# Turning the first inverse by 32x32 blocks on VectorE instead of on TensorE, with GpSimd filling its unit matrices

## The chip, the cores and the metric

The kernel runs on one core of one Trainium2 chip. A core has five engines that work side by side, each through its own list of instructions: TensorE (PE, matrix products, with a separate weight load PEld), VectorE (DVE), ScalarE (ACT), GpSimd (POOL) and SyncE (SP), which here issues the loads. They meet only at semaphores: an instruction may wait for a count and may raise one when it is done. The metric is the device time of one execution in microseconds (us), the median of several.

## The reference

Two transformer blocks run one after the other on a 256 x 1024 input. The change lies in the second block, in its gated delta rule. There each value head, for each block of tokens, needs the inverse of a unit lower triangular matrix:

```python
kb = k * beta[..., None]
A = jnp.where(strict, jnp.einsum('bhntk,bhnsk->bhnts', kb, k) * Lmat, 0.0)
T = lax.linalg.triangular_solve(eye + A, jnp.broadcast_to(eye, A.shape),
                                left_side=True, lower=True, unit_diagonal=True)
u = jnp.matmul(T, v * beta[..., None])
w = jnp.matmul(T, kb * jnp.exp(gam)[..., None])
```

The two blocks are otherwise large matrix products (`w_in`, `ffn` and so on), in single precision.

## The kernel before

Every large product is done on TensorE in three passes. ScalarE writes the high part of a weight chunk (`w_hi`, L655), VectorE the remainder (`w_lo`, L1241), and TensorE multiplies high by high, high by low and low by high. Weights arrive in chunks of 128 x 2048 numbers in a ring of three slots; SyncE refills a slot once `lo_ready` says that it was split.

The second block's heads are worked in a loop, `head(i, gemm, main)`: once for i = 0 without the "main" part, then seven times in a loop that each engine runs for itself (`Fori(1, GH)`), then once more without the "gemm" part. In one pass TensorE computes the projections of head i (24 pieces called `quarter(n)`) and strews between them the small matrix work of head i-1 (`main`). The order on each engine is the order in which the code is written; there is no scheduler.

The inverse is built by doubling. `nt` is the negated strict lower triangle times its decay, for two token blocks and two value heads (128 x 512 numbers together). Level 0 takes from it the pairs directly below the diagonal, the 2x2 blocks:

- VectorE writes four unit matrices into `yi` (L1977), and later, with `copy_predicated` under the mask `lmask[0]`, puts the level-0 entries of `nt` into it (L2007). A `drain` behind it raises `y0_ready` (L2008).
- TensorE waits for `y0_ready` between `quarter(21)` and `quarter(22)` and turns the four 128x128 matrices of `yi` into the PSUM bank `M[:, 5]` (L2967, `t_done`).
- ScalarE copies this bank to `xi` (L1193, `t_ready`) and the diagonal quarters of it to `xc` (L1195, `xc_ready`). Before that it copies quarters of `nt` to `ntc` (L1189, `ntc_ready`).
- VectorE in the meantime, behind L2007, writes the low part of a weight chunk in two halves (L1241), does the prefix sums (L2014), the decayed keys (L2015, L1796), `mt` (L2020), and multiplies the scores into `lt` (L2024), which raises `lt2_ready`. Then it copies the token bank from PSUM (L2028, `evac[1]`).
- At the start of its next pass TensorE waits in `inv_z(1)` for `t_ready`, `ntc_ready` and `lt2_ready` together (L2802 and the lines ahead of it), and its first products read `xi` and `ntc` (L2812).

The steps that lead to L2000 on VectorE, the first of that matrix work: TensorE turns the first mixer's output (L2898); ScalarE works that off (L1154), then key lengths, scaled values, the delta rule's output norm and the query lengths, and the exponential of `lt` (L1165, which waits for `lt_pre` from L1988 on VectorE and raises `lt_ready`); VectorE waits for `lt_ready` at L2000. `vn1_done` is raised by TensorE at L2912, the last product that reads `yi` in a pass.

GpSimd builds masks at the start, writes one `w_lo` chunk halfway, and has nothing else to do.

Of the kernel before, what the change touches and what calls it, by code (L numbers as in the profile page):

```python
# [13 lines left out]
P = 128  # L14
T = 256
TT = T // P
# [67 lines left out]
def emit(nc, ctx, a, out):  # L84
# [3 lines left out]
    def sem(name):  # L88
        return ctx.enter_context(nc.semaphore(name))
# [189 lines left out]
    def quad(ap, side):  # L279
        return ap[HD * side:HD * side + HD, :, :, HD * side:HD * side + HD].rearrange("p i e c -> p (i e) c")  # L280

    def kept(ap, side):
        return ap[HD * side:HD * side + HD, :, :, :].rearrange("p i e c -> p (i e) c")
# [4 lines left out]
    def yh_bank(tile):  # L288
        if tile < 4:
# [62 lines left out]
                         "gbc_ready", "gam_done", "lt_pre", "lt_ready"))  # L352
    qk_done, y0_ready, t_done, t_ready, ffn_step = (
        sem(n) for n in ("qk_done", "y0_ready", "t_done", "t_ready", "ffn_step"))
    zz_done, zc_ready, ww_done, wt_done, xx_ready, yy_ready, yt_done, xc_ready, ntc_ready = (
# [5 lines left out]
        sem(n) for n in ("gsq_ready", "gss_done", "grs_ready", "ogh_ready", "ogl_ready"))  # L361

    gate_tanh = sem("gate_tanh")
    ohh_ready, ohl_ready, ym_ready, ymh_ready, yml_ready = (
# [204 lines left out]
    def _(pool):  # L569
# [55 lines left out]
        for l in range(LEVELS):  # L625
# [5 lines left out]
        nc.gpsimd.tensor_tensor(w_lo[:, slot, :], w_raw[:, slot, :], w_hi[:, slot, :].bitcast(F32), ALU.subtract  # L631
                                ).then_inc(lo_ready, 1)

    BUILT_ID = 3
# [5 lines left out]
    def _(act):  # L640
# [303 lines left out]
        def head(i, gemm, main):  # L944
# [241 lines left out]
            if gemm:  # L1186
                act.wait_ge(y0_ready, i + 1)
                for side in range(2):
                    ins = nc.scalar.activation(kept(ntc, side), quad(nt, side), ACT.Copy)  # L1189
                ins.then_inc(ntc_ready, 1)  # L1190
                act.wait_ge(t_done, i + 1)
                x0 = M[:, 5, :].rearrange("p (i e c) -> p i e c", i=TT, e=2)
                nc.scalar.activation(xi, x0, ACT.Copy).then_inc(t_ready, 1)  # L1193
                for side in range(2):
                    ins = nc.scalar.activation(kept(xc, side), quad(x0, side), ACT.Copy)  # L1195
                ins.then_inc(xc_ready, 1)
                level_exp(1, i + 1)
                level_exp(2, i + 1)
                nc.scalar.activation(n21, nt[:, :, :, HD:P], ACT.Copy)
# [34 lines left out]
    def _(dve):  # L1234
        v = nc.vector

        def settle():
            v.drain()
# [528 lines left out]
        def head(i, gemm, main):  # L1767
# [207 lines left out]
            if gemm:  # L1975
                key_lengths()
                v.tensor_copy(yi, ident[:].unsqueeze(1).unsqueeze(1).to_broadcast([P, TT, 2, P]))  # L1977
            w_low_j(2)
# [16 lines left out]
            if gemm:  # L1995
# [6 lines left out]
                for e in range(2):  # L2002
                    for b in range(TT):
                        v.scalar_tensor_tensor(out=nt[:, b, e, :], in0=kk[:, 2 * b, :], scalar=nbst[:, b, e:e + 1],
                                               in1=lt[:, e, 2 * P * b:2 * P * b + P], op0=ALU.mult, op1=ALU.mult)
                settle()
                v.copy_predicated(yi, lmask[:, 0, :].bitcast(I32).unsqueeze(1).unsqueeze(1).to_broadcast([P, TT, 2, P]), nt)  # L2007
                v.drain().then_inc(y0_ready, 1)  # L2008
                if main:
                    w_low_half(c0 + 3 + RING, 0, i, 6)  # L2010
                    w_low_half(c0 + 3 + RING, 1, i, 6)
# [83 lines left out]
    def _(pe):  # L2095
# [625 lines left out]
        def head(i, gemm, main):  # L2721
# [239 lines left out]
            quarter(21)  # L2961
            if gemm:
                pe.wait_ge(y0_ready, i + 1)
                for b in range(TT):
                    for e in range(2):
                        at = T * b + P * e
                        ins = nc.tensor.transpose(M[:, 5, at:at + P], yi[:, b, e, :], ident[:])  # L2967
                ins.then_inc(t_done, 1)
            quarter(22)
# [79 lines left out]
```

## Time and profile before

| | us |
|---|---|
| median of 3 runs | 1364.0 |
| lowest and highest of them | 1363.79, 1364.14 |
| span of the profiled execution, first to last instruction | 1362.3 |
| PE busy | 1348.9 (99%) |
| DVE busy | 1044.2 (77%) |
| ACT busy | 797.6 (59%) |
| POOL busy | 29.4 (2%) |

The profiled execution's span is 1.7 us below the median time, which also holds what lies around the span. A share of busy time is a mean over all stages. In the timelines a row gives the start in us, the length in us, the engine, the line of the kernel, the operation and its shapes, how many instructions were put together, and in brackets how long the engine was idle before it and who ended that. PE rows carry a modelled end and overlap; the distance from one start to the next tells more than the length. The view of the chain gives each PE piece without that overlap.

### The profile page before, as it was taken

To read this page: it belongs to the slowest core of one execution; us is meant where nothing else is said; L and a number is where in the kernel's file an instruction comes from. 1 tells how busy PE (TensorE), PEld (TensorE's weight loads), DVE (VectorE), ACT (ScalarE), POOL (GpSimd) and SP (SyncE) were. 2 spreads that over 40 slices of the span, in tenths; PEclk is the share of its full clock that TensorE was granted. 3 is DMA by queue.
4 is the path that set the end of the run, shared out by engine and by line. 5 is a ranking of instruction groups with operands and counts; after the bars stand their busy time and mean duration, and the time that the engine had idled before them with its cause. 6 is when DMAs were issued, how large, how long until landed. Compare 5 with 4: busy or idle time off the path is not lost.

```text
span 1362.3 us, 24396 instructions
## 1 busy us (share of the span) xinstructions
PE 1348.9 (99%) x8590; PEld 1210.5 (89%) x8590; DVE 1044.2 (77%) x1644; ACT 797.6 (59%) x1352; POOL 29.4 (2%) x72
## 2 busy tenths in 40 slices
PE   8999999999999999999999999999999999999998
PEld 8888888989888888888899999999999998988887
DVE  5798888777666686666778898898898877666665
ACT  4445554644334364444668898898898853544444
POOL 6000000000000010000000000000000000000000
PEclk9999999999999999999999999999999999999999
DMA  8565555556555756666564444554543286666661
GB/s 267 153 194 153 149 147 160 190 194 206 185 185 187 226 150 209 186 185 185 155 183 136 132 123 131 135 148 115 149 131 123 88 211 203 173 205 197 191 186 62
DMA packets 291214, 227.80 MB, mean 167 GB/s; under 512 B 10882, under 2 KB 270164, under 8 KB 291156
## 3 DMA queue, kind: packets, MB, share of 16 engines
q1 hardware_dynamic: 291012, 226.75, 56.0%
q8 instruction: 38, 0.62, 0.2%
q10 hardware_dynamic: 144, 0.26, 0.1%
q14 instruction: 20, 0.16, 0.0%
HBM read 225.90 MB, written 1.08 MB: 167 GB/s over the span
## 4 chain that ended last, share of the span: by engine, by line
PE 93%; DVE 3%; ACT 1%; issue 1%; DVEq 1%; ACTq 0%; DMA 0%; POOL 0%; SPq 0%; POOLq 0%
PE M L2119 10%; PE G L2119 9%; PE M L2107 7%; PE M L2108 7%; PE M L2109 7%; PE G L2102 5%; PE G L2104 5%; PE G L2103 5%; PE M L2121 5%; PE G L2121 5%; PE G L2245 2%; PE G L3007 2%; PE M L2830 1%; PE M L2812 1%; PE G L3009 1%; PE G L2109 1%
## 5 line engine op out<-in xcount | busy, mean ns | idle before, releaser
L1241 DVE TENSOR_TENSOR w_lo<-w_raw,w_hi 128x2048 fp32r<-128x2048 f32 (+2 forms) x247 | 478.0, 1941 | 126.4 <-ACT w_hi L655 120.6
L655 ACT ACTIVATE w_hi<-w_raw 128x2048 fp32r<-128x2048 f32 x197 | 375.9, 1909 | 169.5 <-PE M L2121 54.3
L2102 PE MATMUL G<-xa,w_hi 128*128 128x256 f32 x592 | 176.9, 299 | 0.0
L2104 PE MATMUL G<-xa,w_lo 128*128 128x256 f32 x592 | 167.3, 283 | 0.0
L2103 PE MATMUL G<-xa,w_hi 128*128 128x256 f32 x592 | 167.0, 282 | 0.0
L2119 PE MATMUL M<-xa,w_hi 128*128 128x512 f32 x600 | 151.6, 394 | 0.0
L2119 PE MATMUL G<-xa,w_hi 128*128 128x512 f32 x568 | 142.4, 393 | 0.0
L2119 PEld LDWEIGHTS M<-xa,w_hi 128*128 128x128 f32 x600 | 107.8, 189 | 19.8
L2119 PEld LDWEIGHTS G<-xa,w_hi 128*128 128x128 f32 x568 | 104.0, 188 | 21.2 <-issue 1.2
L2107 PE MATMUL M<-w_hi,xb 128*128 128x512 f32 x300 | 117.3, 391 | 0.1
L2108 PE MATMUL M<-w_lo,xb 128*128 128x512 f32 x300 | 117.1, 390 | 0.0
L2109 PE MATMUL M<-w_hi,xb 128*128 128x512 f32 x300 | 116.7, 389 | 0.0
L2102 PEld LDWEIGHTS G<-xa,w_hi 128*128 128x128 f32 x592 | 112.9, 191 | 1.4 <-issue 1.3
L2103 PEld LDWEIGHTS G<-xa,w_hi 128*128 128x128 f32 x592 | 112.9, 191 | 0.0
L2104 PEld LDWEIGHTS G<-xa,w_lo 128*128 128x128 f32 x592 | 112.6, 190 | 0.0
L882 ACT ACTIVATE arena<-arena 128x256 f32<-128x256 f32 x38 | 15.9, 418 | 137.9 <-DVE arena L1658 137.9
L2121 PEld LDWEIGHTS M<-xa,w_lo 128*128 128x128 f32 x600 | 81.8, 190 | 5.9
L2121 PE MATMUL M<-xa,w_lo 128*128 128x256 f32 x600 | 83.6, 282 | 0.0
L2121 PEld LDWEIGHTS G<-xa,w_lo 128*128 128x128 f32 x568 | 77.5, 190 | 5.5
L2121 PE MATMUL G<-xa,w_lo 128*128 128x256 f32 x568 | 79.2, 282 | 0.0
L2109 PEld LDWEIGHTS M<-w_hi,xb 128*128 128x128 f32 x300 | 56.3, 188 | 12.0
L2107 PEld LDWEIGHTS M<-w_hi,xb 128*128 128x128 f32 x300 | 56.4, 188 | 11.2 <-issue 0.4
(461 smaller groups left out, 2545.2 us busy)
## 6 DMA issues: line engine op xcount, KB each, us to landing
w_raw<-in_w_in SPq DMA_DIRECT2D x150, 512.0 KB, 4.7
w_raw<-in_ffn_w_in SPq DMA_DIRECT2D x88, 512.0 KB, 5.0
w_raw<-in_w_ff SPq DMA_DIRECT2D x64, 512.0 KB, 4.1
w_raw<-in_ffn_w_out SPq DMA_DIRECT2D x44, 512.0 KB, 4.9
w_raw<-in_w_in SPq DMA_DIRECT2D x33, 256.0 KB, 3.2
w_raw<-in_w_out SPq DMA_DIRECT2D x16, 512.0 KB, 4.1
w_raw<-in_w_branch_gdn SPq DMA_DIRECT2D x16, 512.0 KB, 5.3
w_raw<-in_w_branch SPq DMA_DIRECT2D x12, 512.0 KB, 4.2
```

Of the source, the lines that this page charges most:

```text
L655: nc.scalar.activation(w_hi[:, slot, :], w_raw[:, slot, :], ACT.Copy).then_inc(hi_ready, 1)
L1241: return v.tensor_tensor(dst, src, hi.bitcast(F32), ALU.subtract)
L2102: mm(out_, w[0], x[0], start=first, stop=False)
L2103: mm(out_, w[0], x[1], start=False, stop=False)
L2104: return mm(out_, w[1], x[0], start=False, stop=last_)
L2107: mm(out_, x[0], w[0], start=first, stop=False)
L2108: mm(out_, x[0], w[1], start=False, stop=False)
L2109: return mm(out_, x[1], w[0], start=False, stop=last_)
L2119: mm(both_parts, wh[:, k, at:at + P], xa[:, :, k, :], start=k == 0, stop=False)
L2121: ins = mm(bank[:, 0:T], wl[:, k, at:at + P], xa_hi[:, k, :], start=False, stop=k == KT - 1)
L2245: ins = mm(G[:, j, CW * i:CW * i + CW], x[:, k, P * i:P * i + P], w[j][:, k, :], start=first and k == 0, stop=last and k == KT - 1)
L3007: mm(G[:, n % 2, :].rearrange("p (h t) -> p h t", h=2), wh[:, k, :], xb[:, :, k, :], start=k == 0, stop=False)
```

## The change

It touches the four matrices of level 0 alone.

- On VectorE a `transpose` over the whole 128 x 512 of `yi` writes `xi`, directly behind the drain at L2008. It turns each 32x32 block in its place. Level 0 has entries only inside 2x2 blocks on the diagonal, so the blocks off the diagonal are zero and this is the whole turn. It raises `t_ready`.
- TensorE's four transposes and its wait for `y0_ready` go, and with them ScalarE's copy of the bank to `xi`. ScalarE's copies to `xc` read `xi` in SBUF, and wait for `t_ready`.
- The unit matrices are written by GpSimd for passes 1 to 7, in a loop of its own that waits for `vn1_done`. VectorE waits for the new `yi_ready` ahead of the predicated copy. In pass 0 VectorE still writes them.

```diff
+        with pool.Fori(1, GH) as i:
+            pool.wait_ge(vn1_done, i)
+            pool.sem_inc(waited, 1)
+            nc.gpsimd.tensor_copy(yi, ident[:].unsqueeze(1).unsqueeze(1).to_broadcast([P, TT, 2, P])).then_inc(yi_ready, 1)
...
-                act.wait_ge(t_done, i + 1)
-                x0 = M[:, 5, :].rearrange("p (i e c) -> p i e c", i=TT, e=2)
-                nc.scalar.activation(xi, x0, ACT.Copy).then_inc(t_ready, 1)
+                act.wait_ge(t_ready, i + 1)
                 for side in range(2):
-                    ins = nc.scalar.activation(kept(xc, side), quad(x0, side), ACT.Copy)
+                    ins = nc.scalar.activation(kept(xc, side), quad(xi, side), ACT.Copy)
...
-                v.tensor_copy(yi, ident[:].unsqueeze(1).unsqueeze(1).to_broadcast([P, TT, 2, P]))
+                if not main:
+                    v.tensor_copy(yi, ident[:].unsqueeze(1).unsqueeze(1).to_broadcast([P, TT, 2, P]))
...
                 settle()
+                if main:
+                    dve.wait_ge(yi_ready, i)
+                    dve.sem_inc(waited, 1)
                 v.copy_predicated(yi, lmask[:, 0, :].bitcast(I32).unsqueeze(1).unsqueeze(1).to_broadcast([P, TT, 2, P]), nt)
                 v.drain().then_inc(y0_ready, 1)
+                v.transpose(xi.rearrange("p i e c -> p (i e c)"), yi.rearrange("p i e c -> p (i e c)")).then_inc(t_ready, 1)
...
-            if gemm:
-                pe.wait_ge(y0_ready, i + 1)
-                for b in range(TT):
-                    for e in range(2):
-                        at = T * b + P * e
-                        ins = nc.tensor.transpose(M[:, 5, at:at + P], yi[:, b, e, :], ident[:])
-                ins.then_inc(t_done, 1)
```

On VectorE, in the loop over the heads, from the first wait for `lt_ready` to the low parts of a weight chunk, before the change (arena is the tensor that holds `lt`, `nt`, `yi`, `xi`; line numbers of this kernel):

```order
550 L2000 TENSOR_TENSOR arena<-arena,tri 128x2x2x128 [waits lt_ready]
551 L2004 SCALAR_TENSOR_TENSOR arena<-M,arena 128x128 x4
552 L2007 COPY_PREDICATED arena<-masks,arena 128x512
553 L1252 REGISTER_ALU
554 L1241 TENSOR_TENSOR w_lo<-w_raw,w_hi 128x1024 [waits hi_ready] x2
555 L2014 SCALAR_TENSOR_TENSOR arena<-ones,arena 128x128 [waits lnf_ready]
```

And the same place with the change, whose own line numbers are a few higher:

```order
550 L2005 TENSOR_TENSOR arena<-arena,tri 128x2x2x128 [waits lt_ready]
551 L2009 SCALAR_TENSOR_TENSOR arena<-M,arena 128x128 x4
552 L2015 COPY_PREDICATED arena<-masks,arena 128x512 [waits yi_ready]
553 L2017 STREAM_TRANSPOSE arena<-arena 128x512
554 L1256 REGISTER_ALU
555 L1245 TENSOR_TENSOR w_lo<-w_raw,w_hi 128x1024 [waits hi_ready] x2
```

A wait stands ahead of the predicated copy, and the block transposition stands between it and everything that follows; the copy of the unit matrices, further up, is gone.

On TensorE, in the loop, between `quarter(21)` and `quarter(22)` before the change (the rows that end in 128x512 are products of the token projection):

```order
2303 L2108 MATMUL G<-w_lo,xa 128x512
2304 L2109 MATMUL G<-w_hi,xa 128x512
2305 L2967 MATMUL M<-ident,arena 128x128 [waits y0_ready]
2306 L2967 MATMUL M<-ident,arena 128x128 x3
2307 L2107 MATMUL M<-w_hi,xa 128x512
2308 L2108 MATMUL M<-w_lo,xa 128x512
```

The same place with the change, on to the start of the next pass:

```order
2301 L2117 MATMUL G<-w_lo,xa 128x512
2302 L2118 MATMUL G<-w_hi,xa 128x512
2303 L2116 MATMUL M<-w_hi,xa 128x512
...
2314 L2118 MATMUL M<-w_hi,xa 128x512
2315 L2975 REGISTER_ALU
2316 L2975 COMPARE_AND_BRANCH
2317 L2821 MATMUL M<-arena 128x128 [waits lt2_ready,ntc_ready,t_ready]
```

The four transposes and their wait are gone; twelve products later stands the wait of `inv_z(1)`, unchanged, for three semaphores.

## Rows read from the trace of the kernel before

**Rows 1.** The page: span, and busy time, share and instructions of each engine.
```profile
span 1362.3 us, 24396 instructions
...
PE 1348.9 (99%) x8590; PEld 1210.5 (89%) x8590; DVE 1044.2 (77%) x1644; ACT 797.6 (59%) x1352; POOL 29.4 (2%) x72
```

**Rows 2.** One pass: PE, PEld, DVE, ACT, POOL busy, granted clock, DMA share, GB/s.
```profile
816.27:865.53 49.26, 49.26 (x377) 47.12 (x376) 43.52 (x105) 43.15 (x108) 0.00 (x0) 1.00 0.49 133
```

**Rows 3.** The chain that ended last, in one pass: start, us, engine, line.
```profile
865.88 0.44 PE M L2967 x4
```

**Rows 4.** Timeline of VectorE in the same pass (start, us, engine, line, operation).
```profile
852.32 0.61 DVE L1964 TENSOR_SCALAR arena<-M,arena 128x128 f32<-128x128 f32 x2 [0.41 <-PE M L2912]
852.84 0.28 DVE L1972 TENSOR_SCALAR arena<-arena 128x256 f32<-128x256 f32 x1
...
855.24 0.42 DVE L1977 COPY arena<-ident 128x512 f32<-128x512 f32 x1
855.58 2.28 DVE L1241 TENSOR_TENSOR w_lo<-w_raw,w_hi 128x2048 fp32r<-128x2048 f32 x1
857.78 1.26 DVE L1988 TENSOR_SCALAR arena<-arena 128x128 f32<-128x128 f32 x6
...
860.06 0.69 DVE L2000 TENSOR_TENSOR arena<-arena,tri 128x512 f32<-128x512 f32 x1
860.83 1.13 DVE L2004 SCALAR_TENSOR_TENSOR arena<-M,arena 128x128 f32<-128x128 f32 x4
862.02 0.74 DVE L2007 COPY_PREDICATED arena<-masks,arena 128x512 f32<-128x512 int32 x1
862.96 2.36 DVE L1241 TENSOR_TENSOR w_lo<-w_raw,w_hi 128x1024 fp32r<-128x1024 f32 x2 [0.19 <-issue]
...
867.61 1.02 DVE L2024 SCALAR_TENSOR_TENSOR arena<-M,arena 128x384 f32<-128x384 f32 x2
868.55 0.68 DVE L2028 COPY arena<-G 128x512 f32<-128x512 f32 x1
869.15 0.74 DVE L1740 SCALAR_TENSOR_TENSOR xb<-M,arena,xb 128x512 f32 x1
```

**Rows 5.** Timeline of TensorE's weight loads at the start of the next pass.
```profile
868.22 0.19 PEld L2108 LDWEIGHTS M<-w_lo,xa 128*128 128x128 f32 x1
868.45 0.19 PEld L2109 LDWEIGHTS M<-w_hi,xa 128*128 128x128 f32 x1
868.75 0.57 PEld L2812 LDWEIGHTS M<-arena 128*128 128x128 f32 x4
```

**Rows 6.** Timeline of ScalarE in the same pass.
```profile
855.17 0.47 ACT L1154 ACTIVATE arena<-M,arena 128x256 f32 x1 [0.53 <-PE M L2898]
...
859.18 0.84 ACT L1165 ACTIVATE arena<-arena 128x768 f32<-128x768 f32 x1
...
867.05 0.60 ACT L1193 ACTIVATE arena<-M 128x512 f32<-128x512 f32 x1
```

**Rows 7.** Timeline at the end of pass 0, a row of VectorE and one of TensorE.
```profile
716.18 0.74 DVE L2014 TENSOR_TENSOR_SCAN arena<-ones,arena 128x128 f32<-128x128 f32 x2 [0.55 <-ACT arena L1173]
...
719.85 0.72 PE L2812 MATMUL M<-arena 128*128 128x128 f32 x4 [0.35 <-ACT arena L1193]
```

**Rows 8.** Timeline of VectorE at a wait that stands behind a drain.
```profile
891.43 2.86 DVE L1774 SCALAR_TENSOR_TENSOR arena<-arena 128x256 f32<-128x256 f32 x6
894.54 0.31 DVE L1827 COPY_PREDICATED arena<-masks,M 128x128 f32<-128x128 int32 x1 [0.26 <-issue]
```

**Rows 9.** Groups of GpSimd's instructions by line: operation, count, busy us, mean ns.
```profile
L602 POOL TENSOR_SCALAR_AFFINE_SELECT arena<-arena 128x256 f32<-128x256 f32 x1 | 0.4, 409 | 0.0
```

**Rows 10.** Timeline at the kernel's start, one row of VectorE and two of GpSimd.
```profile
14.47 2.29 DVE L1241 TENSOR_TENSOR w_lo<-w_raw,w_hi 128x2048 fp32r<-128x2048 f32 x1 [2.92 <-ACT w_hi L655]
...
13.57 0.35 POOL L622 TENSOR_SCALAR_AFFINE_SELECT masks<-masks 128x64 f32<-128x64 f32 x1
...
14.51 2.46 POOL L622 TENSOR_SCALAR_AFFINE_SELECT masks<-masks 128x64 f32<-128x64 f32 x1
```

More of the change, by code:

```diff
@@ L352, in emit @@
                          "gbc_ready", "gam_done", "lt_pre", "lt_ready"))
-    qk_done, y0_ready, t_done, t_ready, ffn_step = (
-        sem(n) for n in ("qk_done", "y0_ready", "t_done", "t_ready", "ffn_step"))
+    qk_done, y0_ready, t_ready, ffn_step = (
+        sem(n) for n in ("qk_done", "y0_ready", "t_ready", "ffn_step"))
     zz_done, zc_ready, ww_done, wt_done, xx_ready, yy_ready, yt_done, xc_ready, ntc_ready = (
@@ L361, in emit @@
         sem(n) for n in ("gsq_ready", "gss_done", "grs_ready", "ogh_ready", "ogl_ready"))
+    yi_ready = sem("yi_ready")
     gate_tanh = sem("gate_tanh")
```

## The prediction

> **What bounds the kernel now.** I read the page first. TensorE is busy for 99% of the span [rows 1], so only what lengthens or shortens TensorE's own sequence moves the time. The windows say the same of the heads' loop: one pass lasts 49.26 us and TensorE is busy for all of it, VectorE for 43.5 and ScalarE for 43.2, at a granted clock of 1.00, the level of 2.4 GHz [rows 2]. The list of waits has no entry for TensorE between 767 and 1064 us. A busy TensorE seems to promise that any work taken off it is time gained. The second question is what stands right behind it, and that is asked at the waits which TensorE meets after the place of the change. There is one, 3 us later: the start of the next pass, where L2812 needs `t_ready`, `ntc_ready` and `lt2_ready`.
>
> Look at how near that wait is. VectorE ends L2024, which raises `lt2_ready`, at 867.61 + 1.02 = 868.63 [rows 4]. TensorE's weight loads run at a distance of 0.23 us (868.22, 868.45), and the next one, the first of L2812, starts at 868.75, which is 0.30 behind the one before and 0.12 behind the end of L2024 [rows 5]. It came 0.07 us later than the rhythm asks for; the products did not notice, since a weight load is ahead of its product. So the pass has no cover at this wait. TensorE is as busy as it can be, and VectorE's chain to `lt2_ready` is equally long to within a tenth of a us. This is the row on which my forecast rests.
>
> Then follow that chain back to where TensorE starts it. VectorE runs from L2000 at 860.06 to 868.63 without an idle gap over 0.2 us [rows 4]. L2000 waits for `lt_ready`, raised by ScalarE's L1165, which ends at 859.18 + 0.84 = 860.02 [rows 6], 0.04 ahead. ScalarE has been working without a gap since L1154 at 855.17, and there it had idled 0.53 us for TensorE's L2898 [rows 6]. So from L2898 to L2812 two things run side by side: TensorE's own products, and a chain ScalarE, then VectorE, of the same length.
>
> **The change, part by part.**
>
> *TensorE.* Four transposes go in each pass. The chain gives them 0.44 us together [rows 3]. They are inside the stretch from L2898 to L2812. If nothing else held TensorE, it would reach L2812 0.44 us earlier in each of passes 1 to 7, 3.1 us in all. In pass 0 TensorE idled at L2812 anyway (0.35 by the row) for ScalarE's L1193 [rows 7], so there the four transposes cost nothing before.
>
> *ScalarE.* L1193 goes, 0.60 us [rows 6], and the copies to `xc` read SBUF. Its place is at 867.05, behind L1165; nothing in the chain to `lt2_ready` comes after it. It hides under TensorE before and after: I cost it at zero.
>
> *VectorE, the copy of the unit matrices.* It goes from 855.24, and what follows starts 0.34 us earlier (855.58 - 855.24) [rows 4]. But L2000 waits for ScalarE, which ended only 0.04 before; the gain stops there. Worth at most 0.04 us a pass on the chain; I take 0.
>
> *VectorE, the new wait.* Behind a drain, the predicated copy now has a wait and a semaphore instruction ahead of it. Before, it starts 0.06 us after L2004's end (860.83 + 1.13 = 861.96, 862.02) [rows 4]. The nearest row with drain, wait and semaphore instruction is L1827: it starts 0.25 after L1774's end (891.43 + 2.86 = 894.29, 894.54) [rows 8], which has a register computation too. So the wait costs 0 to 0.19; I take 0.10.
>
> *VectorE, the transposition.* The trace has none. Other instructions over 128x512 numbers bound it. L2028 occupies VectorE for 0.60 us (868.55 to 869.15), the predicated copy lasts 0.74 [rows 4]. The lower end is half of L1241's 2.36/2 = 1.18 us for 1024 columns, 0.59. If a block had to be filled before it can be emptied, it could be twice 0.60. I take 0.60 as it reads one operand and writes one, like L2028. Of the 0.19 us of issue before L1241 [rows 4] a part, some 0.11, is register work that can now run under the transposition. In sum the low parts of the weights and all that follows start 0.10 + 0.60 - 0.11 = 0.59 us later.
>
> The Trainium skill, page "VectorE: DVE Perf Modes", section "Rules for kernel authors", calls the DVE transposition the fastest for 32x32 blocks, and its section "The three transpose paths" gives 311 ns against TensorE's 390 for 128x128 in bf16. Taken as advice the change should win; it says nothing of which engine stands on the path.
>
> *What queues behind it.* Two halves of L1241, L2014, L2015, L1796, L2020, L2024, L2028. Of these `lt2_ready` (L2024) has no cover. `evac[1]` (L2028) is needed by L2756 behind L2812 and moves with it.
>
> *GpSimd.* Its copy starts when L2912 is done, about 852.3 (VectorE's L1964 waits for the same) [rows 4]. By its 0.41 us for 128x256 [rows 9] it lasts at most 0.82. The predicated copy wants the result at 862.0, 9 us later, so the wait itself is met. What it might disturb is VectorE at L1972 (852.84). That GpSimd and VectorE do stop each other the start of the kernel shows: an instruction that takes GpSimd 0.35 us took 2.46 next to VectorE's L1241 of 2.29 us, and ended with it [rows 10]. Were VectorE held instead, from 852.84 to at most 853.2, it would lose 0.3 us, against the 0.34 it gains by the missing copy; `lt_pre` (L1988 ends 859.04, wanted by ScalarE at 859.18) [rows 4, 6] then comes no later. I cost it at 0.
>
> The Trainium skill, page "SBUF — State Buffer", section "Who interferes with whom", makes this an exclusive lock on a shared pair of ports, held for the whole instruction by whoever starts first. The two rows agree in size; that VectorE is the one to be held no row of before shows.
>
> *The sum.* In a pass the chain from L2898 to L2812 grows by 0.59, less the hundredths with which TensorE's weight load has play, say 0.57. TensorE's own way gets 0.44 shorter, so it arrives early and waits about 1.0 us; the pass as a whole lasts 49.26 + 0.57. Beyond L2812 both engines are shifted alike. Passes 1 to 7: 7 x 0.57 = 4.0 us. Pass 0: before, VectorE waited 0.55 us for ScalarE behind the predicated copy [rows 7], so the transposition is covered, and TensorE loses its wait for L1193 but not for `lt2_ready`: 0. The span becomes 1362.3 + 4.0 = 1366.3, and with the 1.7 us around it **1368.0 us**. The bounds: 0 for the wait and 0.59 for the transposition give 0.48 a pass less 0.05, 3.0 us in all; 0.19 and 0.74, with nothing hidden, give 0.93, 6.5 us.
>
> **The rivals.**
>
> *TensorE keeps the lead (faster).* If the nearness at L2812 is chance and the chain has play of more than 0.6 us that the rows do not show (for instance the weight load is always sent just in time), the pass shortens by 0.44: 1364.0 - 3.1 = 1360.9. For it: TensorE shows no idle row in the loop. Against it: weight load and L2024 stand 0.12 us apart and the load was late.
>
> *A draw.* If the chain gives up part of its 0.59, by an instruction of VectorE that waited in a way the idle column hides under 0.15 us, the growth falls under 0.39 a pass. Then the time is within 0.2% (2.7 us, about what a measurement of this kernel can tell from no change): about 1365.5.
>
> *Dearer yet (slower).* The transposition takes 1.2 us, or GpSimd's copy lasts 1.4 us (the 5.6 us that its 128x2048 subtraction took, by length) and holds VectorE's L1972 to 853.8. The first adds 0.6 a pass. The second delays L1972 by about 1.0 and `lt_pre` to 859.7 where 859.18 was wanted, adding 0.5. Either gives 1368.0 + 3.5 to 4.2 = about 1372.
>
> **How the numbers follow.** Forecast, 1366.8 to 1370.5: 0.68. TensorE keeps the lead: 0.10. A draw: 0.13. Dearer: 0.09. So faster by over 0.2% has 0.10, within 0.2% 0.13, slower by over 0.2% 0.77. The range goes from 1364.8 to 1370.8: it leaves out the first rival, a part of the draw and most of the dearer case, 0.2 together.
>
> **What would show it.** In the profile after, a pass of 49.8 us. L2812's weight load (its new line) starts about 0.1 us behind the end of the `lt` product, as now, and TensorE has an idle gap of about 1 us before it, put down to VectorE, in seven passes. The transposition has rows of about 0.6 to 0.7 us, and the predicated copy starts 0.1 later after its drain. ScalarE's exponential still ends just before L2000. I am wrong if the pass is 48.8 us with no gap before L2812 (then the chain had play), or if VectorE's L1972 or `lt_pre` come later by half a us (then GpSimd is the cause).

## The result, and the profile after

The change makes the kernel slower: the median of seven runs is 1367.95 us (1367.28 to 1368.38), that of the kernel before, run beside it, 1363.79 (1363.54 to 1364.17). The ratio is 1.003, with a 95% interval of 1.0021 to 1.0039. The profiled execution has a span of 1365.6 us, 3.3 more than before.

The page of the kernel after, its span, the busy time of each engine, and the shares of the chain that ended last:

```profile
span 1365.6 us, 24368 instructions
...
PE 1345.9 (99%) x8558; PEld 1206.7 (88%) x8558; DVE 1048.6 (77%) x1645; ACT 793.8 (58%) x1344; POOL 33.7 (2%) x79
...
PE 89%; DVE 4%; ACT 3%; DVEq 2%; issue 1%; ACTq 0%; POOL 0%; POOLq 0%
```

TensorE has 32 instructions and 3.0 us of work less than in [rows 1], and the span is 3.3 us longer. The busy share is still 99% and does not show what happened; the chain gives TensorE 89% where it gave it 93% before. The window of the pass that [rows 2] shows, here from one first inverse product to the next:

```profile
820.30:870.17 49.87, 49.05 (x371) 46.72 (x372) 44.06 (x105) 42.71 (x106) 0.62 (x1) 1.00 0.49 131
```

The pass grew from 49.26 to 49.87 us, and TensorE is no longer busy for all of it (49.05). At the start of the pass it now stands still, as its timeline shows:

```profile
868.96 0.39 PE L2118 MATMUL M<-w_hi,xa 128*128 128x512 f32 x1
870.17 0.69 PE L2821 MATMUL M<-arena 128*128 128x128 f32 x4 [0.82 <-DVE arena L2033]
```

From the last projection product to the first product of the inverse 1.21 us pass, where the rhythm is 0.23. The releaser is L2033, the old L2024, which raises `lt2_ready`. The list of waits of the kernel after has it with 6.6 us in eight places (the end of pass 0 and of the seven passes behind it), 0.9 us the longest:

```profile
PE M L2821 <- DVE arena L2033: 6.6, 8, 0.9
```

The weight load of that product is again 0.12 us behind the end of the `lt` product (869.00 + 1.02 = 870.02), as in [rows 5]. Of the other two semaphores `ntc_ready` was raised at 867.8 and `t_ready` at 864.5. First the load, then VectorE's timeline from L1968 (L1964 before) to the `lt` product:

```profile
870.14 0.53 PEld L2821 LDWEIGHTS M<-arena 128*128 128x128 f32 x4 [1.22 <-issue]
```

```profile
853.07 0.61 DVE L1968 TENSOR_SCALAR arena<-M,arena 128x128 f32<-128x128 f32 x2 [0.42 <-PE M L2921]
853.60 0.37 DVE L1976 TENSOR_SCALAR arena<-arena 128x256 f32<-128x256 f32 x1
853.88 0.59 DVE L1750 SCALAR_TENSOR_TENSOR arena<-M,arena 128x128 f32<-128x128 f32 x2
...
860.80 0.69 DVE L2005 TENSOR_TENSOR arena<-arena,tri 128x512 f32<-128x512 f32 x1
861.57 1.13 DVE L2009 SCALAR_TENSOR_TENSOR arena<-M,arena 128x128 f32<-128x128 f32 x4
862.88 0.75 DVE L2015 COPY_PREDICATED arena<-masks,arena 128x512 f32<-128x512 int32 x1 [0.18 <-issue]
863.74 0.71 DVE L2017 STREAM_TRANSPOSE arena<-arena 128x512 f32<-128x512 f32 x1
864.38 2.32 DVE L1245 TENSOR_TENSOR w_lo<-w_raw,w_hi 128x1024 fp32r<-128x1024 f32 x2
...
869.00 1.02 DVE L2033 SCALAR_TENSOR_TENSOR arena<-M,arena 128x384 f32<-128x384 f32 x2
```

The view of the chain that ended last, in this pass, goes from TensorE's L2907 (L2898 before) through ScalarE and VectorE back to TensorE. Before the change it ran on TensorE alone here, as in [rows 3]:

```profile
855.56 0.23 PE M L2907 x2
...
855.92 0.47 ACT arena L1160
...
860.04 0.74 ACT arena L1171
860.80 0.69 DVE arena L2005
...
869.00 0.22 DVE arena L2033
...
870.17 0.69 PE M L2821 x4
```

From L2009's start to the low parts of the weights (L1245) 2.81 us pass, against 2.13 before (862.96 - 860.83 in [rows 4]). The 0.68 more are made up of 0.12 by the wait ahead of the predicated copy (0.18 instead of 0.06 behind the end of the instruction before), 0.64 by the transposition, less 0.08 of issue time that lay before L1245 and is now hidden. The end of the `lt` product is 14.63 us behind the start of L2907's product, against 13.99 before: 0.64 more, since the rest of the stretch is 0.04 shorter.

On ScalarE, the exponential that [rows 6] shows at 859.18 stands here:

```profile
859.93 0.84 ACT L1171 ACTIVATE arena<-arena 128x768 f32<-128x768 f32 x1
```

It ends 0.03 us before VectorE's L2005 starts, as before 0.04. What follows on VectorE starts at the same place of the pass as before (within 0.01 us behind L2898), although the copy of the unit matrices is gone.

GpSimd's copy of them, the one new row on that engine:

```profile
853.20 0.62 POOL L638 COPY arena<-ident 128x512 f32<-128x512 f32 x1 [49.26 <-PE M L2921]
```

**Where the 3.3 us of the spans come from.** Up to the first product of the inverse at the end of pass 0 the execution after is 0.59 us ahead (719.26 against 719.85); 0.64 of this lies before the change acts at all, so pass 0 costs 0.05. From there to the same product at the end of pass 7 it takes 350.38 us against 346.11, 4.27 more, 0.61 a pass. What follows is 0.38 shorter. 4.27 + 0.05 - 0.64 - 0.38 = 3.3. The medians, 4.16 apart, are nearer to the seven passes alone. Why the execution was 0.64 ahead at the start, and why the stretch behind the last pass is shorter, was not followed.

### The profile page after: what moved, and what is told of

Read it like the earlier page. It is cut to its first block, busy times and chain, and to the rows that moved or that the text cites. A ratio compares the mean times of both kernels' runs of the same rounds, so it can differ in the third digit from the quotient of the medians.

```text
span 1365.6 us, 24368 instructions
## 1 busy us (share of the span) xinstructions
PE 1345.9 (99%) x8558; PEld 1206.7 (88%) x8558; DVE 1048.6 (77%) x1645; ACT 793.8 (58%) x1344; POOL 33.7 (2%) x79
## 4 chain that ended last, share of the span: by engine, by line
PE 89%; DVE 4%; ACT 3%; DVEq 2%; issue 1%; ACTq 0%; POOL 0%; POOLq 0%
PE M L2128 10%; PE G L2128 10%; PE M L2116 7%; PE M L2117 7%; PE M L2118 7%; PE G L2111 5%; PE M L2130 5%; PE G L2113 5%; PE G L2112 5%; PE G L2130 5%; PE G L2254 2%; PE G L3009 2%; DVEq L1242 1%; PE M L2821 1%; PE M L2839 1%; PE G L3011 1%
## 5 line engine op out<-in xcount | busy, mean ns | idle before, releaser
L1245 DVE TENSOR_TENSOR w_lo<-w_raw,w_hi 128x2048 fp32r<-128x2048 f32 (+2 forms) x247 | 477.9, 1941 | 124.8 <-ACT w_hi L661 120.6
```

The source lines that it names most:

```text
L1245: return v.tensor_tensor(dst, src, hi.bitcast(F32), ALU.subtract)
```

## The experiments

The theory: from L2898 to L2812 a chain of ScalarE and VectorE is as long as TensorE's own work, so whatever lengthens VectorE's part comes out one for one, and what is taken off TensorE's part is worth nothing. The rivals: the missing transposes move something else on TensorE (its order, its loads); GpSimd's copy or the wait for it is the whole cause; or another wait than the one for `lt2_ready` holds TensorE. All ratios are to the kernel before, run on the same chip. All edits touch the heads' loop alone.

**Half a transposition.** In passes 1 to 7 only one of the two token blocks is turned; the other half of `xi` keeps old numbers, so this kernel leaves out a part of the inverse.

```diff
-                v.transpose(xi.rearrange("p i e c -> p (i e c)"), yi.rearrange("p i e c -> p (i e c)")).then_inc(t_ready, 1)
+                if main:
+                    v.transpose(xi[:, 0].rearrange("p e c -> p (e c)"), yi[:, 0].rearrange("p e c -> p (e c)")).then_inc(t_ready, 1)
+                else:
+                    v.transpose(xi.rearrange("p i e c -> p (i e c)"), yi.rearrange("p i e c -> p (i e c)")).then_inc(t_ready, 1)
```

> The changed kernel, but in passes 1 to 7 VectorE turns only the first token block of yi, 128x256 numbers in place of 128x512; the second block of xi keeps old numbers, so part of the inverse is left out. Theory (the block transposition lies on VectorE's chain to lt2_ready, and that chain sets the pass): the transposition becomes 256 columns shorter, 0.27 us by the rate of other VectorE rows (1.14 us for 1024 columns), and the pass falls from 49.87 to 49.60, in all 7 x 0.27 = 1.9 us less than the changed kernel. Rival 1 (GpSimd's copy in VectorE's way, or the new wait, makes the loss): no change, 49.87. Rival 2 (TensorE's stall has another releaser than VectorE): no change.

Measured: 1366.09 us, ratio 1.0016 (1.0007 to 1.0025); the pass 49.59 us. The view of one line, first for the kernel after and then for this one (the three numbers are the shortest, median and longest in ns):

```profile
L2017 DVE STREAM_TRANSPOSE arena<-arena x8: 712/712/714, 715.1 to 1063.2; 128x512 f32<-128x512 f32 x8
```

```profile
L2018 DVE STREAM_TRANSPOSE arena<-arena x7: 445/447/448, 764.6 to 1062.3; 128x256 f32<-128x256 f32 x7
```

0.265 us less in each of seven transpositions, and a pass 0.28 shorter: one for one. Counted from the kernel before, the loss fell from 4.16 to 2.38 us, by 1.8, where 1.9 was expected. (The rate named in the expectation, 1.14 us for 1024 columns, gives 0.285 for 256, not 0.27.)

**TensorE's transposes put back as dead work.** They write the bank that nobody reads, with their wait for `y0_ready`; everything else as after.

```diff
             quarter(21)
+            if gemm:
+                pe.wait_ge(y0_ready, i + 1)
+                for b in range(TT):
+                    for e in range(2):
+                        at = T * b + P * e
+                        nc.tensor.transpose(M[:, 5, at:at + P], yi[:, b, e, :], ident[:])
             quarter(22)
```

> The changed kernel with TensorE's four transposes of yi and their wait put back at their old place; nobody reads what they write. Theory (TensorE arrives about 1 us early at the start of the next pass, so its own work there is free): the pass stays 49.87 and the time that of the changed kernel within 0.5 us; the gap ahead of the first inverse product falls by 0.44. Rival (TensorE's transposes have a price, and taking them off saved their 0.44 a pass): pass 50.3, 3.1 us over the changed kernel.

Measured: 1367.65 us, ratio 1.003 (1.0018 to 1.0041), the pass 49.87, the same as after. TensorE's timeline, the transposes and the first product of the next pass, and its wait there:

```profile
867.35 0.60 PE L2976 MATMUL M<-ident,arena 128*128 128x128 f32 x4
...
871.06 0.70 PE L2821 MATMUL M<-arena 128*128 128x128 f32 x4 [0.36 <-DVE arena L2033]
```

```profile
PE M L2821 <- DVE arena L2033: 3.0, 8, 0.4
```

The gap shrank from 0.82 to 0.36 us, by about what the transposes take, and the pass did not get longer. So the 0.44 us that the change takes off TensorE is converted whole into waiting.

**The unit matrices back on VectorE.** No GpSimd, no `yi_ready`, no wait; the transposition stays.

```diff
-        with pool.Fori(1, GH) as i:
...
-                if not main:
-                    v.tensor_copy(yi, ident[:].unsqueeze(1).unsqueeze(1).to_broadcast([P, TT, 2, P]))
+                v.tensor_copy(yi, ident[:].unsqueeze(1).unsqueeze(1).to_broadcast([P, TT, 2, P]))
...
-                if main:
-                    dve.wait_ge(yi_ready, i)
-                    dve.sem_inc(waited, 1)
```

> The changed kernel without GpSimd's part: VectorE writes the unit matrices as before and the predicated copy has no wait ahead of it. Theory (the copy of 0.34 us lies under ScalarE's exponential, the new wait costs the 0.12 us seen between the two profiles): the pass falls from 49.87 to 49.75, 0.8 us in all below the changed kernel. Rival (GpSimd blocks VectorE on a port and this is the loss): the pass falls by 0.4 or more, 3 us in all. If the copy's 0.34 were on the path instead, the pass would rise by 0.2.

Measured: 1367.12 us, ratio 1.0025 (1.0015 to 1.0036), the pass 49.76, 0.11 less than after. VectorE's timeline:

```profile
853.94 0.28 DVE L1971 TENSOR_SCALAR arena<-arena 128x256 f32<-128x256 f32 x1
...
861.91 1.12 DVE L2003 SCALAR_TENSOR_TENSOR arena<-M,arena 128x128 f32<-128x128 f32 x4
863.11 0.75 DVE L2006 COPY_PREDICATED arena<-masks,arena 128x512 f32<-128x512 int32 x1
```

The predicated copy is 0.08 us behind the end of the instruction before it, not 0.18. Giving the 0.42 us copy back to VectorE costs nothing, and dropping the wait gains 0.11 a pass: the part of the change that looks like free relief is the smaller of its two losses. It also ends the rival that GpSimd is the whole cause.

**The GpSimd part alone, on the kernel before.** It uses `mck_ready`, which the kernel has raised before for something else; the count to wait for is a sum with the loop's number, and that puts a register computation ahead of the wait.

```diff
+        with pool.Fori(1, GH) as i:
+            pool.wait_ge(vn1_done, i)
+            pool.sem_inc(waited, 1)
+            nc.gpsimd.tensor_copy(yi, ident[:].unsqueeze(1).unsqueeze(1).to_broadcast([P, TT, 2, P])).then_inc(mck_ready, 1)
...
+                if not main:
+                    v.tensor_copy(yi, ident[:].unsqueeze(1).unsqueeze(1).to_broadcast([P, TT, 2, P]))
...
+                if main:
+                    dve.wait_ge(mck_ready, i + PAIRS + 1)
+                    dve.sem_inc(waited, 1)
```

> The kernel before with GpSimd's part alone: GpSimd writes the unit matrices, VectorE waits for them ahead of the predicated copy, and the transposes stay on TensorE. Theory (the wait costs 0.12 on a chain without cover, the copy of 0.34 saves nothing): the pass goes from 49.27 to 49.39 less what play the weight load has (0.03), 0.6 to 0.9 us in all over the kernel before. Rival (the copy's absence shortens the chain): 49.27 or less.

Measured: 1365.65 us, ratio 1.0012 (1.0003 to 1.0022), the pass 49.52; 49.36 to 49.39 was expected. VectorE's timeline:

```profile
861.50 1.13 DVE L2010 SCALAR_TENSOR_TENSOR arena<-M,arena 128x128 f32<-128x128 f32 x4
862.88 0.75 DVE L2016 COPY_PREDICATED arena<-masks,arena 128x512 f32<-128x512 int32 x1 [0.26 <-issue]
```

With the register computation the copy starts 0.25 us behind, 0.19 later than before, which is what L1827 of [rows 8] shows for the same sequence. The `lt` product ends 0.29 later, and the pass is 0.25 longer. The size was missed for one part because the edit's wait is not the change's. The other 0.10 stands directly ahead of the `lt` product: VectorE is idle there for 0.18 us by the row, put down to issue, where the kernels before and after have 0.08 and 0.09. The direction stands; what makes the 0.10 is open. The kernels below that have both the transposition and moved low parts show the same 0.18; the two that move low parts on the kernel before show 0.08.

```profile
868.57 1.02 DVE L2033 SCALAR_TENSOR_TENSOR arena<-M,arena 128x384 f32<-128x384 f32 x2 [0.18 <-issue]
```

These four and the two kernels give one line. The pass against the end of the `lt` product, counted from the start of L2898 in pass 3:

| kernel | end of `lt` product | pass | difference |
|---|---|---|---|
| before | 13.99 | 49.27 | 35.28 |
| GpSimd part alone | 14.28 | 49.52 | 35.24 |
| half a transposition | 14.37 | 49.59 | 35.22 |
| unit matrices on VectorE | 14.52 | 49.76 | 35.24 |
| after | 14.63 | 49.87 | 35.24 |
| dead transposes | 14.64 | 49.87 | 35.23 |

The slope is 1: from the `lt` product's end on, the five kernels that wait there need the same 35.22 to 35.24 us. The play that the kernel before had at this wait is 35.28 - 35.24, some 0.04 us.

**Giving the chain cover.** If VectorE's chain to `lt2_ready` is shortened, TensorE should lead, and then the 0.44 us should count. The second half of the low-part write (some 1.2 us) can go behind the token copy, past `lt2_ready`.

```diff
                     w_low_half(c0 + 3 + RING, 0, i, 6)
-                    w_low_half(c0 + 3 + RING, 1, i, 6)
...
                 if main:
+                    w_low_half(c0 + 3 + RING, 1, i, 6)
                     delta_out_low(i)
```

> The changed kernel with the second half of the weight chunk's low part (L1245, 1.14 us) moved on VectorE from behind the transposition to behind the copy of the token bank, that is behind lt2_ready and evac[1]. Theory: lt2_ready comes 1.14 us earlier, more than the 1.0 us that TensorE waits, so TensorE leads again and the pass is 49.26 - 0.44 = 48.82; against the changed kernel 7 x 1.05 = 7.3 us less, against the one before about 3.1 us less (1360.8). Rival (the moved half is itself needed at once: lo_ready at 869.9 in the frame of the pass before, wanted by TensorE at 870.1): a new wait at the low product of the next chunk, pass between 48.9 and 49.3, no gain over the kernel before.

Measured: 1368.65 us, ratio 1.0036 (1.0022 to 1.005), the pass 49.93. This expectation failed: 48.82 was forecast, and the pass is longer than the changed kernel's. TensorE's timeline and its list of waits, and VectorE's timeline, at the start of the pass:

```profile
870.21 0.63 PE L2821 MATMUL M<-arena 128*128 128x128 f32 x4
...
875.67 0.61 PE L2821 MATMUL M<-arena 128*128 128x128 f32 x3 [0.83 <-DVE arena L1844]
```

```profile
PE M L2821 <- DVE arena L1844: 5.3, 7, 0.9
```

```profile
873.76 1.22 DVE L1245 TENSOR_TENSOR w_lo<-w_raw,w_hi 128x1024 fp32r<-128x1024 f32 x1
874.90 0.72 DVE L1844 COPY_PREDICATED arena<-masks,M 128x256 f32<-128x256 int32 x1
```

The wait for `lt2_ready` is gone, and the next product of the inverse has one of the same size, for VectorE's copy between two levels (L1844). VectorE does not end its chain at `lt2_ready`: it runs on to the second and third level, with one pause (0.56 us, put down to issue, behind L1744). The work was only moved from ahead of one release to ahead of the next. The theory of one chain and one wait was too small; the same chain meets TensorE several times. The trace of the kernel before has it already. VectorE's copies between the levels (L1840) end there at 873.13 and 877.43, and TensorE's weight loads that need them start 0.08 and 0.20 us later, 4.5 and 8.9 us behind the first. VectorE's rows, then the loads:

```profile
872.40 0.73 DVE L1840 COPY_PREDICATED arena<-masks,M 128x256 f32<-128x256 int32 x1
...
876.70 0.73 DVE L1840 COPY_PREDICATED arena<-masks,M 128x256 f32<-128x256 int32 x1
```

```profile
873.21 0.54 PEld L2812 LDWEIGHTS M<-arena 128*128 128x128 f32 x4
...
877.63 0.53 PEld L2812 LDWEIGHTS M<-arena 128*128 128x128 f32 x4
```

**Cover at the second meeting too.** The first half of the next chunk goes behind that copy (`inverse(1)`).

```diff
-            if main and gemm:
-                w_low_half(c0 + 4 + RING - 6, 0, i, 6)
             inverse(1)
...
             if main and gemm:
+                w_low_half(c0 + 4 + RING - 6, 0, i, 6)
                 w_low_half(c0 + 4 + RING - 6, 1, i, 6)
```

> The changed kernel with two pieces of VectorE's order moved: the second half of one weight chunk's low part from behind the transposition to behind the token bank's copy (as in the run before), and the first half of the next chunk's low part from ahead of inverse(1) to behind it. The run before showed that the first move only carries the wait on to the second inverse product, where TensorE waits for inverse(1)'s predicated copy (L1844, 875.64 there). Theory (VectorE's whole run from lt_ready to inverse(1) is the chain, and only work moved past both waits shortens it): both waits go, TensorE leads, the pass is 48.85 to 49.0, and the time 2 to 3 us under the kernel before (about 1361.2). Rival 1 (VectorE is short of time as a whole, so the wait comes back further on, at low parts or at level 2 of the inverse): pass 49.3 or more, not faster than before. Rival 2 (the earlier lt2_ready is worth nothing, since ScalarE's chain holds it): pass as in the changed kernel, 49.87.

Measured: 1368.38 us, ratio 1.0033 (1.0021 to 1.0046), the pass 49.82, again a miss. TensorE's timeline and waits:

```profile
880.12 0.61 PE L2820 MATMUL M<-arena 128*128 128x128 f32 x3 [0.53 <-DVE arena L1844]
```

```profile
PE M L2820 <- DVE arena L1844: 3.9, 8, 0.5
```

Now the third product waits, 0.5 us. Two more kernels have the same two moves.

> As the run with both pieces moved, but VectorE writes the unit matrices itself and the predicated copy has no wait. Theory: on a pass that TensorE leads, the 0.12 us of the wait has cover, so within 0.05 us a pass of that run; if lt2_ready is still a little late there, up to 0.12 a pass and 0.8 us in all less. Rival (VectorE short of time as a whole): 0.34 a pass more, 2.4 us in all, since its copy comes back.

With the unit matrices on VectorE (the edit of above added): 1367.78 us, ratio 1.0029 (1.0018 to 1.004), the pass 49.71, 0.11 less than with GpSimd's, near the top of what was expected (0 to 0.12).

> The kernel before, transposes on TensorE and all, with the same two pieces of VectorE's order moved. Theory (TensorE's own work and the chain were equally long there, so a shorter chain alone frees nothing): pass 49.27 as before, time within 0.5 us of it. Rival (the two moves are a gain by themselves, whoever does the transposition): pass under 49.1, over 1 us less than before.

The same moves on the kernel before: 1369.02 us, ratio 1.0038 (1.0024 to 1.0052), the pass 50.05; 49.27 was expected, a miss. VectorE's timeline and TensorE's waits there:

```profile
874.20 0.75 DVE L1840 COPY_PREDICATED arena<-masks,M 128x256 f32<-128x256 int32 x1 [0.85 <-PE M L2829]
```

```profile
PE M L2811 <- DVE arena L1840: 3.7, 7, 0.5
```

The moves took away what VectorE did while it waited for TensorE's product: it idles 0.85 us, and lacks the time at the third meeting, where TensorE waits 0.5 us. Such a filler delays what is behind it and uses the wait ahead of it, both at once.

**Three moves.** The first half of the chunk after next goes behind `inverse(2)` too, so that all three meetings have cover.

```diff
+            inverse(2)
             if main and gemm:
                 w_low_half(c0 + 5 + RING - 6, 0, i, 6)
-            inverse(2)
```

Once with the unit matrices on VectorE, once on GpSimd, and once on the kernel before, all on one chip:

> Block transposition on VectorE, unit matrices by VectorE (no GpSimd, no wait), and three halves of low parts moved: the two of the runs before, and the first half of the chunk after next from ahead of inverse(2) to behind it. The last runs showed the wait carried on from the first to the second and third inverse product with each move (inverse(2)'s copy, 0.5 us late there). Theory (VectorE's run from lt_ready to inverse(2) is the chain; behind inverse(2) VectorE idles about 1 us for ScalarE, so work moved there is hidden): no wait left at the three products, TensorE leads, and its missing transposes count at last: pass 48.83, 7 x 0.44 = 3.1 us under the kernel before, 1360.7. Rival (VectorE is short further on too): a wait at the fourth product or at a low part, pass 49.3 or more.

> The same three halves moved in the changed kernel as it is, with GpSimd's unit matrices and the wait for them. Theory: the wait's 0.12 us has cover now, since lt2_ready comes 1.1 us earlier: pass 48.83 to 48.85, within 0.3 us of the run with VectorE's unit matrices. Rival: the 0.12 still counts, 0.8 us more.

> The kernel before, four transposes on TensorE, with the same three halves moved. It tells the moves' own worth apart from the transposition's. Theory: TensorE's work alone was 49.26 us a pass, so with cover at every wait the pass is 49.25 to 49.27, the kernel before's time within 0.5 us, and 3.1 us over the same order with the block transposition. Rival (the moves are themselves the gain): 1361 too.

| kernel | us | ratio (95%) | pass |
|---|---|---|---|
| three moves, transposition, units on VectorE | 1362.21 | 0.9988 (0.9979 to 0.9997) | 48.94 |
| three moves, transposition, units on GpSimd | 1363.04 | 0.9994 (0.9985 to 1.0003) | 49.03 |
| three moves on the kernel before | 1363.72 | 1.0 (0.9991 to 1.0009) | 49.27 |

The window of one pass of the last of them:

```profile
868.86:918.13 49.27, 49.27 (x377) 47.18 (x375) 43.60 (x105) 43.13 (x108) 0.00 (x0) 1.00 0.49 133
```

TensorE is busy for all 49.27 us: the moves alone are worth nothing, and the transposition alone cost 0.6 a pass. Together they are worth 0.33 of the 0.44 us that four transposes take. With the units on GpSimd the time can't be told from the kernel before (the interval holds 1). With the units on VectorE 48.83 had been expected; 0.12 is lost at one place, where a score product (L2788) comes late in TensorE's timeline, for an instruction of the scores in VectorE's. The three rows are of TensorE's products, of its weight loads and of VectorE:

```profile
874.52 0.49 PE L2788 MATMUL M<-arena 128*128 128x128 f32 x2
```

```profile
874.52 0.30 PEld L2788 LDWEIGHTS M<-arena 128*128 128x128 f32 x2
```

```profile
874.05 0.42 DVE L1819 TENSOR_TENSOR arena<-M,ident 128x256 f32<-128x256 f32 x1
```

L1819 ends at 874.47 and raises `sc_used`, for which L2788 waits; its weight load starts 0.05 us later, at the same time as its product, where a load is otherwise 0.12 ahead. On GpSimd the units cost 0.09 a pass more, by TensorE's starts at two places, a product that reads a low part (L2769) and this one, 0.05 to 0.06 each. The expectation that the wait would have cover there failed: the two medians are 0.83 us apart, and its rival said 0.8.

**The scores between the halves.** So `scored(0)` goes ahead of the second half, with the unit matrices on VectorE:

```diff
             if main and gemm:
-                w_low_half(c0 + 4 + RING - 6, 1, i, 6)
+                w_low_half(c0 + 4 + RING - 6, 0, i, 6)
             scored(0)
+            if main and gemm:
+                w_low_half(c0 + 4 + RING - 6, 1, i, 6)
```

> The order with three halves moved and VectorE's unit matrices, and in it the level-0 scores (scored(0)) taken up between the two halves of the next chunk's low part. The run before had a pass of 48.93 where 48.83 was worked out, and TensorE's one late start there was the level-2 product, 0.12 us, which waits for sc_used from scored(0), ending 0.06 us ahead of it. Theory: scored(0) comes 1.1 us earlier, the gap goes, pass 48.81 to 48.84, a further 0.1 a pass: about 1361.5 and 2.4 us under the kernel before. Rival (the second half of the low part, now 0.4 us later, is waited for): pass 48.93 or more.

Measured: 1361.42 us against 1363.66, ratio 0.9982 (0.9973 to 0.9991), the pass 48.80. The window of one pass, and a row of the list of TensorE's waits:

```profile
868.04:916.84 48.80, 48.80 (x372) 46.78 (x371) 44.10 (x106) 42.65 (x108) 0.00 (x0) 1.00 0.50 134
```

```profile
PE G L2622 <- DVE w_lo L1240: 0.6, 1, 0.6
```

TensorE is busy without a gap again, and the pass is 0.47 us shorter than before: 0.44 of the transposes and 0.03. TensorE's starts are those of the kernel before, to 0.03 us, up to the place of the four transposes, so the whole gain lies there. Seven such passes would make 3.3 us. The profiled executions give 3.1 over the seven (342.97 us against 346.11), and lose again 0.4 ahead of them and 0.6 behind; there, in the last pass, which the moves were not made for, TensorE waits 0.6 us for a low part (L2622), which the list of the kernel before does not have. The spans differ by 2.1, the medians by 2.2. This kernel beats both: the one before by 2.2 us (the interval leaves out 1, though the gain is under 0.2%) and the one after, counted from the kernel before, by 6.4. The fourth move was not tried on the kernel before, where TensorE had no gap left to close.

## Why the prediction was right

1368.0 us was forecast, 1367.95 measured, and for the reason given. By its steps:

- *TensorE and the chain are equally long at L2812.* Shown. The weight load that came 0.07 us later than the rhythm was the one sign in the trace of before, and 0.04 us of play is what the series of kernels gives.
- *The transposition occupies VectorE for 0.60.* It occupies 0.64 from start to start, and lasts 0.71. The nearest row, an instruction with one operand over as many columns (L2028, 0.60 to the next start), was good to 0.04; the lower bound, half of L1241, was too. The choice of row was good luck in part. [rows 4] has another instruction over 128x512 with one operand, the copy L1977, which reads and writes SBUF as the transposition does and takes 0.34 to the next start; L2028 reads PSUM. Priced by L1977 the sum would have been 0.31 a pass and 1366.2 us, and the prediction does not say why it passed over that row, though it calls 0.59 the lower end.
- *The wait costs 0.10.* 0.12 by the row, 0.11 by the kernel without it. The upper bound of 0.19, from L1827 with its register computation, is met by the kernel that has such a computation, 0.19.
- *0.11 of issue is hidden under the transposition.* 0.68 more from L2009 to L1245, where 0.12 and 0.64 would be 0.76: 0.08 hidden there.
- *Sum 0.57 a pass, 4.0 us.* 0.60 a pass between the products of pass 3, 0.61 as a mean of seven; 4.3 us.
- *TensorE's 0.44 is worth nothing; it waits 1.0 us.* Shown by the dead transposes; 1.21 - 0.23 = 0.98.
- *ScalarE's missing copy and the missing copy of the unit matrices are worth 0.* Shown: L2005 starts at the same place, behind ScalarE. With the copy back on VectorE nothing is lost.
- *GpSimd's copy is in time and disturbs VectorE by less than the 0.34 gained.* It lasts 0.62, under the bound of 0.82. L1976 beside it lasts 0.37 instead of 0.28, and the next instruction starts 0.28 instead of 0.20 behind: VectorE loses 0.08 us. The nearest row had allowed 0.3.
- *Pass 0 costs 0.* 0.05. The transposition was not wholly covered: the `lt` product starts 0.16 later (718.09 + 0.64 against 718.57), and TensorE, 0.88 us idle, waits for it.

That the sum came within 0.05 us is luck. The seven passes gave 0.3 us more than forecast, the growth of the medians was 4.16 and not 4.0, and the kernel before, run beside the changed one, was 0.2 faster than the 1364.0 that the forecast started from.

What the prediction did not see, and did not need, is that VectorE's chain does not end at `lt2_ready`. It named the one wait 3 us behind the change and took it for the last link. The two expectations on giving the chain cover failed on just that: behind that wait come two more, 4.5 and 8.9 us later in the kernel before, nearly as tight (0.08 and 0.20 us). Play made at `lt2_ready` alone, by that reordering, did not let the time fall as the prediction's first rival has it.

The Trainium skill, page "VectorE: DVE Perf Modes", section "Rules for kernel authors", names VectorE the fastest for 32x32 blocks. In this case's rows that depends on what is counted. As an engine's time it is not: four matrices take 0.71 us on VectorE and 0.44 on TensorE, in fp32. As a path it is: behind TensorE's 0.44 came ScalarE's copy out of PSUM, 0.60 us [rows 6], which the block transposition does without. The last experiments use it with profit, once VectorE's time at that place is not on the path; the cost of the edit was set by where it stood and not by its length alone.

The Trainium skill, page "SBUF — State Buffer", section "Who interferes with whom", describes the lock between VectorE and GpSimd as exclusive. This trace fits that, and does not prove it. VectorE's L1976 starts at 853.60, while GpSimd's copy runs from 853.20 to 853.82, and ends at 853.97, 0.15 us behind the copy; so it does, to 0.01, in all seven passes. Of the 0.28 us that it takes undisturbed some 0.14 is a fixed part, by an estimate from two instructions inside SBUF in [rows 4], though of different kinds (0.28 for L1972's 128x256, 0.42 for L1977's 128x512). An instruction held until 853.82, with its other 0.14 to come, would end at 853.96 too. The GpSimd instruction of [rows 10] likewise ended 0.2 us behind the VectorE instruction that held it, and not its own 0.35. Read so, the disturbance is only 0.1 us here because L1976 started late in the copy.

## What to carry to other kernels

When the busiest engine is at 99%, ask which of its waits is met with almost no play, and look at the weight load or issue just before it: here a load 0.07 us late said that another engine's chain was as long, work moved onto that chain cost its full length, and work taken off the busy engine was worth nothing. The late load is a sign and not the test: at the next two waits of the kernel before the loads come in rhythm, and only the distance from the end of the releasing instruction, 0.08 and 0.20 us, tells how near the chain is. A chain that feeds such an engine can meet it again further on, and then cover must be made at every meeting before the saving shows; here it took three moves of other work, worth nothing on the kernel before, one more, and GpSimd's part taken back, to turn +4.2 us into -2.2. A handover to an idle engine is not free either: its wait stands on the engine that you meant to relieve.

## What the runs showed of the hardware

- A 32x32 block transposition on VectorE in fp32 takes 0.447 us for 128x256 and 0.712 for 128x512: 1.03 ns a column, about 0.18 us fixed. That is about as long as a copy of that size out of PSUM (L2028, 0.68), longer than a copy inside SBUF (L1977, 0.42), and not the 1.2 us of the prediction's dearer case.
- A wait and a semaphore instruction between a drain and the next VectorE instruction cost 0.12 us here, though the semaphore had been raised 9 us before; with a register computation for the count 0.19.
- A GpSimd copy of 128x512 in fp32 takes 0.617 us and stretched a VectorE instruction that started 0.4 us after it by 0.09; at the start of the kernel a GpSimd instruction that started 0.04 us after one of VectorE's was held for 2 us [rows 10]. In both the one that started later ended 0.15 to 0.2 us behind the other. That the rest of the other's length makes the difference fits both and was not tried apart.
- An engine that is 100% busy over a pass can be just as fast as a chain beside it. In the kernel before there was 0.04 us between the two over the 14 us from L2898 to L2812, and nothing in busy shares or idle columns tells it.
